# Splitting the branch, output, gate and down projections of a two-block transformer kernel into high and low parts

## What is computed

```python
# first block, each of 2 layers (x: 256 x 1024)
h = x @ w_in                                  # for three attention branches a, b, c
ya, yb, yc = moba(...), mla(...), diff(...)   # 256 x 512 each, gated with silu of a part of h
g = sigmoid(x @ w_m + b_m)                    # 1024 x 3072
merged = ga * (ya @ w_a) + gb * (yb @ w_b) + gc * (yc @ w_c)      # w_a, w_b, w_c: 512 x 1024
out = merged @ w_o                            # 1024 x 1024
r = ALPHA * x + out
r = r + sigmoid(r @ w_pg) * (p_i @ w_p)       # w_pg: 1024 x 1024
x = layernorm(r)
# second block, each of 2 layers
x = x + hybrid_mixer(rmsnorm(x))              # convolutions, a state space scan, w_in_2, w_out_2
x = x + (silu(h @ w_gate) * (h @ w_up)) @ w_down     # layer 0: dense FFN, w_down: 2816 x 1024
x = x + moe(h)                                # layer 1: top 2 of 8 experts
```

## Time and profile before

| | |
|---|---|
| time, median of 3 runs | 2277.96 us (2274.99 to 2281.9) |
| profiled execution | 2279.82 us, span of its trace 2277.6 us |
| TensorE matmul busy | 2223.8 us, 98% of the span |
| VectorE, ScalarE, GpSimd busy | 1355.2, 1200.6, 455.5 us |
| mean granted TensorE clock | 0.984 of full speed |

### The profile page before, as it was taken

How to read it: one execution, slowest core, us unless ns; L and a number is a source line. 1 busy time by engine, 2 the same in 40 slices (tenths; PEclk the granted TensorE clock), 3 DMA queues, 4 the chain that set the end, 5 groups by cost and what they waited for, 6 DMA issues and landing times.

```text
span 2277.6 us, 32486 instructions
## 1 busy us (share of the span) xinstructions
PE 2223.8 (98%) x12804; PEld 1953.8 (86%) x12804; DVE 1355.2 (60%) x1365; ACT 1200.6 (53%) x1296; POOL 455.5 (20%) x224
## 2 busy tenths in 40 slices
PE   9999999999999999999998999999999999999997
PEld 8979998988998898999897888888888888888885
DVE  1454212335311693000593898998989898989895
ACT  4456213455421543222442676777777676767673
POOL 6626412725530201445300000000000000000000
PEclk9999999999999999999998999999999999999998
DMA  7434444615444334545435798999999999999992
GB/s 233 123 113 144 151 163 147 184 44 177 148 156 148 121 104 132 180 148 186 133 110 185 283 371 326 378 354 348 371 326 368 334 373 329 369 329 374 358 352 101
DMA packets 306510, 528.26 MB, mean 232 GB/s; under 512 B 11376, under 2 KB 152336, under 8 KB 306416
## 3 DMA queue, kind: packets, MB, share of 16 engines
q1 hardware_dynamic: 306224, 526.44, 66.2%
q0 software_dynamic: 192, 0.48, 0.1%
HBM read 525.84 MB, written 1.05 MB: 231 GB/s over the span
## 4 chain that ended last, share of the span: by engine, by line
PE 86%; issue 5%; DVE 3%; POOL 3%; ACT 2%; DMA 1%; DVEq 0%; POOLq 0%; ACTq 0%
PE bank L631 83%; POOL weights_low L2516 2%; PE bank L1242 1%; DVE qb L1873 1%; ACT sc L1344 1%; DVE sc L1873 1%; PE bank L783 0%; DMA ring<-in_w_out_dram 0%; ACT weights_high L1347 0%; PE bank L686 0%; DVE h L1881 0%; DVE expert_weights_low L1873 0%; DMA ring<-in_ffn_w_up_dram 0%; DVE sc L1881 0%; ACT expert_weights_high L1347 0%
## 5 line engine op out<-in xcount | busy, mean ns | idle before, releaser
L1873 DVE TENSOR_TENSOR expert_weights_low<-ring_experts,expert_weights_high 128x2048 fp32r<-128x2048 f32 x336 | 765.2, 2289 | 94.1 <-ACT expert_weights_high L1347 93.5
L1347 ACT ACTIVATE expert_weights_high<-ring_experts 128x2048 fp32r<-128x2048 f32 x336 | 645.4, 1922 | 176.9 <-PE bank L631 176.9
L2516 POOL TENSOR_TENSOR weights_low<-ring,weights_high 128x1024 fp32r<-128x1024 f32 x176 | 429.7, 2468 | 629.8 <-ACT weights_high L1347 629.8
L1347 ACT ACTIVATE weights_high<-ring 128x1024 fp32r<-128x1024 f32 x216 | 221.2, 1054 | 381.0 <-PE bank L631 122.2
L631 PE MATMUL bank<-expert_weights_high,gathered_high 128*128 128x512 f32 x896 | 356.6, 398 | 1.4 <-DVE gathered_low L1873 1.4
L631 PE MATMUL bank<-expert_weights_high,gathered_low 128*128 128x512 f32 x896 | 349.4, 390 | 0.0
L631 PE MATMUL bank<-x_high,weights_high 128*128 128x256 f32 x896 | 256.4, 288 | 0.9 <-POOL weights_low L2516 0.9
L631 PE MATMUL bank<-x_low,weights_high 128*128 128x256 f32 x896 | 250.2, 285 | 0.0
L631 PE MATMUL bank<-x_high,weights_low 128*128 128x256 f32 x896 | 249.7, 280 | 0.0
L631 PE MATMUL bank<-expert_weights_low,gathered_high 128*128 128x512 f32 x896 | 239.7, 389 | 0.0
L631 PE MATMUL bank<-h_high,weights_high 128*128 128x256 f32 x704 | 202.7, 290 | 6.3 <-ACT h_high L1347 6.3
(11 more groups left out here) (264 smaller groups left out, 3136.5 us busy)
## 6 DMA issues: line engine op xcount, KB each, us to landing
ring_experts<-in_moe_w_gate_dram SPq DMA_DIRECT2D x112, 1024.0 KB, 6.4
ring_experts<-in_moe_w_up_dram SPq DMA_DIRECT2D x112, 1024.0 KB, 6.2
ring_experts<-in_moe_w_down_dram SPq DMA_DIRECT2D x112, 1024.0 KB, 5.8
ring<-in_w_in_dram SPq DMA_DIRECT2D x62, 1024.0 KB, 5.3
ring<-in_w_merge_dram SPq DMA_DIRECT2D x24, 1024.0 KB, 5.2
ring<-in_w_out_dram SPq DMA_DIRECT2D x16, 1024.0 KB, 5.1
ring<-in_ffn_w_gate_dram SPq DMA_DIRECT2D x11, 1024.0 KB, 5.4
ring<-in_ffn_w_up_dram SPq DMA_DIRECT2D x11, 1024.0 KB, 5.5
```

The costliest lines, as they stand in the source:

```text
L1347: return nc.scalar.activation(dst, src, ACT.Copy, scale=scale)
L1873: return nc.vector.tensor_tensor(dst, x, z, op)
L2516: nc.gpsimd.tensor_tensor(half_of(wlo[:, q_slot, :], t), half_of(ring[:, slot, :], t), half_of(whi[:, q_slot, :], t).bitcast(F32), ALU.sub ...
```

## The change

Six more kinds of weights become split units: `w_a`, `w_b`, `w_c`, `w_out`, `w_pg` of both layers and `ffn_w_down_2`. That is 14 units a layer and 11 in the FFN, 39 together. Their activations are split too: `y` into `yh`, `yl`; `merged` into `mh`, `ml`; `r1` into `xh`, `xl`; the hidden tile into `hfh`, `hfl`. `w_out_2` of the mixer stays plain. The core of the diff, with its new functions:

```diff
-          + [f"{z}z{n}" for z in "abc" for n in range(2)] + [f"mg{j}" for j in range(12)])
+          + [f"{z}z{n}" for z in "abc" for n in range(2)]
+          + [x for c, br in enumerate("abc") for x in [f"mg{4 * c + j}" for j in range(4)] + [f"b{br}0", f"b{br}2"]]
+          + [f"ou{j}" for j in range(4)] + [f"pg{j}" for j in range(4)])
-KINDS1 = [["split" if name in ("w_in", "w_merge") and cols == 256 else "plain" for name, _, cols, _ in units]
+SPLIT_WEIGHTS = ("w_in", "w_merge", "w_a", "w_b", "w_c", "w_out", "w_pg")
+KINDS1 = [["split" if name in SPLIT_WEIGHTS and cols in (256, 512) else "plain" for name, _, cols, _ in units]
...
-        kinds2 = ["split" if cols == 256 and name in ("w_in_2", "ffn_w_gate_2", "ffn_w_up_2") else "plain"
+        kinds2 = ["split" if name in ("w_in_2", "ffn_w_gate_2", "ffn_w_up_2", "ffn_w_down_2") and cols != 8 else "plain"
...
+            def split_half(b, half, slot, lo_at, x, count):
+                wh, wl = (w[:, slot, :].rearrange("p (k n) -> p k n", n=512) for w in (whi, wlo))
+                pe.wait_ge(lo_done.h, lo_at + half)
+                for t in range(2):
+                    cols = slice(half * S + t * P, half * S + (t + 1) * P)
+                    for kk in range(4):
+                        mm(views(b)[:, t, :], wh[:, kk, cols], x[0][:, kk, :], kk == 0, False)
+                        mm(views(b)[:, t, :], wh[:, kk, cols], x[1][:, kk, :], False, False)
+                        ins = mm(views(b)[:, t, :], wl[:, kk, cols], x[0][:, kk, :], False, kk == 3)
...
-                        project(name, w[:, :, 256 * (j % 2):256 * (j % 2) + 256], y[:, 4 * c:4 * c + 4, :], 4)
+                        split_half(begin(name), j % 2, *halves)
+                    elif name == "ou0":
+                        split_project_first(begin(name), *take_split(name, (mh, ml)),
+                                            lambda j: pe.wait_ge(mh_ready.h, mh_ready.at(layer, j + 1)),
+                                            lambda j: pe.wait_ge(ml_ready.h, ml_ready.at(layer, j + 1)))
+                    elif name == "pg0":
+                        split_project_first(begin(name), *take_split(name),
+                                            lambda j: pe.wait_ge(rh_ready.h, rh_ready.at(layer, j + 1)),
+                                            lambda j: pe.wait_ge(rl_ready.h, rl_ready.at(layer, j + 1)))
...
+            def down(slot, lo_at, h_at, x):
+                wh, wl = (w[:, slot, :].rearrange("p (k n) -> p k n", n=D) for w in (whi, wlo))
+                for half in range(2):
+                    pe.wait_ge(lo_done.h, lo_at + half)
...
+                            mm(views(4 + t // 2)[:, half, :], wh[:, kk, cols], hfh[:, x, kk, :], False, False, share=True)
...
ACT, in split1: what frees a half of a weight slot
+                    if half_width(before) == S:
+                        other = half_width((SPLIT1 + SPLIT1)[q]) != S
+                        G1.wait_full(act, turn, before[:2] + str(int(before[2]) + (1 if other else t)))
+                    elif half_width((SPLIT1 + SPLIT1)[q]) == S:
+                        G1.wait_full(act, turn, before)
...
ACT
+                def branch_high(n, c):
+                    act.wait_ge(gated.h, gated.at(layer, n))
+                    copy(yh[:, part, :], y[:, part, :]).then_inc(y_high.h, 1)
+                def pair_high(dst, src, ready, n, done, j):
+                    act.wait_ge(ready.h, ready.at(layer, n))
+                    copy(dst[:, 2 * j:2 * j + 2, :], src[:, 2 * j:2 * j + 2, :]).then_inc(done.h, 1)
...
+                after("bc0", (0,))
+                pair_high(mh, merged, mgd, 5, mh_ready, 0)
+                after("bc0", (1,))
+                pair_high(mh, merged, mgd, 6, mh_ready, 1)
+                after("bc2", (0,))
+                pair_high(mh, merged, mgd, 7, mh_ready, 2)
+                pair_high(mh, merged, mgd, 8, mh_ready, 3)
+                after("bc2", (1,))
                 for j in range(4):
+                    if j:
+                        after(f"ou{j - 1}", (1,))
+                    if j < 3:
+                        after(f"ou{j}", (0,))
                     drain(layer, f"ou{j}", ou[:, 2 * j:2 * j + 2, :], 0.5)
+                    if j:
+                        pair_high(xh, r1, r_ready, j, rh_ready, j - 1)
+                pair_high(xh, r1, r_ready, 4, rh_ready, 3)
+                after("ou3")
...
DVE
+                def pair_low(dst, src, high, ready, done, j):
+                    dve.wait_ge(ready.h, ready.at(layer, j + 1))
+                    tt_(dst[:, pair, :], src[:, pair, :], high[:, pair, :].bitcast(F32), ALU.subtract).then_inc(done.h, 1)
...
                         tt_(dst, dst, u, ALU.add).then_inc(mgd.h, 1)
+                        if c == 2 and j:
+                            pair_low(ml, merged, mh, mh_ready, ml_ready, j - 1)
+                    if c == 0:
+                        branch_low(3, 1)
+                pair_low(ml, merged, mh, mh_ready, ml_ready, 3)
...
DVE, FFN
-                stt(hf[:, half], tb[:, half], 0.5, views(b + 1), ALU.mult, ALU.mult).then_inc(ff_h.h, 1)
+                stt(hf[:, half], tb[:, half], 0.5, views(b + 1), ALU.mult, ALU.mult).then_inc(ff_raw.h, 1)
+                dve.wait_ge(ff_raw.h, step)
+                nc.vector.tensor_copy(hfh[:, half], hf[:, half]).then_inc(ff_high.h, 1)
+                dve.wait_ge(ff_high.h, step)
+                tt_(hfl[:, half], hf[:, half], hfh[:, half].bitcast(F32), ALU.subtract).then_inc(ff_h.h, 1)
```

More of the change, by code:

```diff
@@ L236, with half_of, half_width @@
           + [(f"wo{j}", "v") for j in range(4)])
-def half_of(unit, t):
-    return unit.rearrange("p (k t n) -> p t k n", t=2, n=P)[:, t]
+def half_of(unit, t, n=P):
+    return unit.rearrange("p (k t n) -> p t k n", t=2, n=n)[:, t]
+def half_width(name):
+    return S if name[:2] in ("ba", "bb", "bc") else P
 def quarter(unit, k):
@@ L723, in take_split @@
                     assert SPLIT1[q] == name
-                    return q % 2, lo_done.at(layer, 2 * q + 1), (xh, xl), full
+                    return q % 2, lo_done.at(layer, 2 * q + 1), x, full
                 def begin(name):
@@ L897, in layer_body @@
                         if j % 2 == 0:
[L898 removed]
+                            halves = take_split(name, (yh[:, 4 * c:4 * c + 4, :], yl[:, 4 * c:4 * c + 4, :]))
                         if j == 0:
[L900 to L907 removed]
+                            pe.wait_ge(y_split.h, y_split.at(layer, {"a": 1, "c": 2, "b": 3}[name[1]]))
+                        split_half(begin(name), j % 2, *halves)
[7 more added lines that the diff above has]
+                                            lambda j: pe.wait_ge(rl_ready.h, rl_ready.at(layer, j + 1)))
+                    elif name[:2] == "ou":
+                        split_project(begin(name), *take_split(name, (mh, ml)))
                     elif name in ("lm", "lv"):
                         b = begin(name)
[L910 removed]
                         src, ready = (merged, r2_ready) if name == "lm" else (sq, ln_sq)
@@ L1116, in norm, with take_down @@
                     pe.wait_ge(nrm["h"].h, n - 1)
[L1118 to L1124, removed]
+            def down(slot, lo_at, h_at, x):
+                wh, wl = (w[:, slot, :].rearrange("p (k n) -> p k n", n=D) for w in (whi, wlo))
+                for half in range(2):
+                    pe.wait_ge(lo_done.h, lo_at + half)
+                    if half == 0:
+                        pe.wait_ge(ff_h.h, h_at)
+                    for t in range(half, DT, 2):
+                        cols = slice(t * P, (t + 1) * P)
+                        for kk in range(2):
+                            mm(views(4 + t // 2)[:, half, :], wh[:, kk, cols], hfh[:, x, kk, :], False, False, share=True)
+                            mm(views(4 + t // 2)[:, half, :], wh[:, kk, cols], hfl[:, x, kk, :], False, False, share=True)
+                            ins = mm(views(4 + t // 2)[:, half, :], wl[:, kk, cols], hfh[:, x, kk, :], False, False,
+                                     share=True)
+                    ins.then_inc((used if half == 0 else ff_down).h, 1)
+            def take_down(x, step):
+                slot, lo_at, _, _ = take_split(ff_down)
+                down(slot, lo_at, step, x)
             def clear_sums():
@@ L1347, in copy, with split @@
                 return nc.scalar.activation(dst, src, ACT.Copy, scale=scale)
-            def split(slot, landed_at, q_slot, free, halves=(0, 1)):
+            def split(slot, landed_at, q_slot, free, halves=(0, 1), width=P):
                 act.wait_ge(landed[slot].h, landed_at)
@@ L1374, in free @@
                         G1.wait_full(act, turn, before)
-                split(n % RING, 16 * (n // RING + 1), q % 2, free, halves)
+                split(n % RING, 16 * (n // RING + 1), q % 2, free, halves, half_width((SPLIT1 + SPLIT1)[q]))
             def drain(layer, name, dst, scale=1.0, rows=slice(0, P)):
```

161 lines of the change are left out of this document (108 added, 53 removed).

## The result

The changed kernel takes 2243.25 us in the median of 4 runs (2242.33 to 2248.41), the kernel before 2276.59 beside it: a ratio of 0.9854, 95% interval 0.9832 to 0.9877. The forecast was 2242, the range 2230 to 2264. The profiled execution is the longest of the four, 2248.41 us with a span of 2246.6.

A forecast was written before the change was run, and what follows sets the result against it. TensorE's own work was taken as the bound: 2279.8 - 45.8 saved on PE + 10 of new waits = 2244.0 us for the profiled execution, 2242 in the median. Range 2230 to 2264 us.

The forecast's parts named there:

- The bound and the price of a block: PE's own work sets the time; a block costs 431.7 ns plain, 359.7 (layers) or 354.9 (FFN) split; 45.8 us less.
- the 119.9 ns: Price of one fp32r matmul, read from mg8 to mg11 (192 in 23.02 us); three make a split block, 359.7 ns.
- The price by four passes and three quarters: All plain matmuls: three products cost three quarters of float32's four passes, 67.3 us less, 2221 us; chance 0.02.
- What is given back: PE waits at three places a layer as DVE and POOL exclude each other: 5 us a layer, 10 both, bounds 0 and 16.
- ou0: First output unit: PE waits for its weights and the last pair of merged, 3 us a layer.
- the walk with the two engines in turn: Wait at the first output unit, walked through with measured durations, DVE and POOL alternating: 3 to 4 us.
- pg0: First gate unit: its second weight half and the chain from ou3 come late, between 0 and 2, taken as 1 us.
- The end of the gate groups: Two DVE operations after pg3 meet POOL on the next layer's first weights: between 0 and 2.4, taken as 1 us.
- B, collisions that fall well: POOL and DVE miss each other at the three places, PE waits about 1 us in all, 2233 us; chance 0.18.
- C, POOL as the bound: From bc0 to pg3 POOL's halves pace the units, up to 21 us over 20 units, 2250 to 2264 us; chance 0.20.
- D: Slower: POOL halves above 3.45 us in all 39 units; at 4 us each, 43 us slower, 2320 us; chance 0.06.
- E: No measurable difference: POOL halves of 3.3 to 3.5 us, 2271 to 2285 us; chance 0.04.

The follow-up runs named there:

- port_free: Changed kernel with DVE's two-SBUF-tile operations from the last branch to the gate groups reading a bank instead (other values computed); bc0 to norm's sums 57.7 us against 62.9.
- the fillers: Changed kernel with 6 and 3 bf16 matmuls of zeros before PE's waits for high pairs 2 and 3 of merged; 2236.64 us, ratio 0.9834.
- lows_last: Changed kernel with DVE making the low parts of merged behind its last add of bc3, not between the adds; 2236.48 us, ratio 0.9817.
- copies_first: Changed kernel with ACT copying pairs 2 and 3 of merged before it splits ou1's first weight half; 2246.72 us, ratio 0.987.

## Why the prediction was right, point by point

**The bound and the price of a block** held. TensorE's work set the time. The FFN gained 13.3 us (forecast 13.5). In the layers, with the waits taken out (`ou0` to `pg0` in `port_free`, the rest in the changed kernel, `bc0` to `ou0` less 1.02 us of waiting for weights), each gained 2.46 + 2.45 + 2.45 + 4.84 + 4.90 = 17.1 us, 34.2 for both against 32.3. That term was 2 us too small: the 119.9 ns were read over a stretch that begins just behind plain matmuls, with a first one of 0.47 us. Behind split units the same four gate units take 22.83 us instead of 23.02, and a whole branch unit pair 11.36 us, 118.3 ns a matmul. Together 47.5 us instead of 45.8. The price by four passes and three quarters, the rival at 2221 us, is excluded: a loop turn of split units alone takes 34.08/288 = 118.3 ns a matmul.

**What is given back** was the right mechanism, in the right places, and too small: 10 us forecast with bounds of 0 and 16, and 18.1 measured in the profiled execution, outside its own bounds.
- `ou0`: 3 us a layer forecast; 1.0 for the weights and 4.9 in the output groups (27.70 - 22.79) measured, 5.9. The waits themselves are 3.5 us, within what the walk with the two engines in turn gave (3 to 4). Another 1.5 us is the half clock on 24 matmuls, which the sum did not have at all; the fillers gave 1.4 of it back. The rest, some 0.9 us, is slower starts behind each wait and the wait before `pg0`.
- `pg0`: 1 us a layer forecast, 0.3 measured, before its first matmul; it is contained in the 4.9 above.
- The end of the gate groups: 1 us a layer forecast; 0.6 in layer 0, but 2.8 + 2.7 in layer 1. There two units are split ahead and not one, so POOL is at work through DVE's last operations: the pair before the last ends 1 us late, and the last operation of all takes 2.71 us instead of 0.69. Behind that the clock halves again, and this is the whole of the second 2.7: the 16 squares take 6.23 us instead of 3.53. A window of the changed kernel in layer 1:

```profile
730.00:735.00 5.00, 5.00 (x13) 3.97 (x12) 0.47 (x1) 2.42 (x3) 0.00 (x0) 0.50 0.12 7
```

So the half clock, which stood nowhere in the sum, is 1.5 + 1.5 + 2.7 = 5.7 of the 18.1 us. With the port taken out (`port_free`) the clock stayed up and the same stages gave back only 1.7 us: nearly all of the loss comes of DVE's lateness at the port, directly or by the clock behind it.

**Why the total came out** nearly exact all the same: the profiled execution is 31.0 us shorter in its span. Of this -47.5 + 18.1 = -29.4 are the change's, where the forecast had -45.8 + 10 = -35.8. The start took 3.0 us more, mixer 0 and 1 took 4.3 and 0.9 less, the experts 0.6 more. The second execution of the same kernel has its start at 228.66 and its mixer at 161.47, so these are chance. The agreement of the medians to 1 us is luck: two terms were off by 2 and 8 us, which together is 6.4 us too much gain, and executions of one kernel differ by more than that.

**The rivals.** B, collisions that fall well, did not come: four operations in a row were held up, in both layers and in both executions, so it is the program's order and not luck. C, POOL as the bound, did not either: its median is 2.40 us, its longest 3.41 as before, and PE waits for low weights 0.8 us by name and 2.1 us under `issue`. It was near, though: from 324.39 POOL did six halves without a pause in 16.00 us, 5.33 a unit against PE's 5.7. The FFN stayed at PE's pace with a margin that was used: `hidden_low` took 2.8 to 2.9 us in each step. D and E are excluded by the interval.

## What to carry to other kernels

A helper engine that was idle is a cover like any other: when POOL is given work all the time, each VectorE operation on two SBUF tiles may cost 2 to 3 us instead of 0.7, and those on the way to the next matmul should be counted one by one, with the order in which the two engines meet. Put such operations behind the ones that somebody waits for, or let them read a bank. Look where they go: moved behind the norm, POOL's work met DVE's scaling and nothing was won. And price a wait of TensorE with the clock it may cost behind it, which here was 1.5 us behind waits of 3.5.

## What the runs showed of the hardware that was not expected

- Behind three waits of 0.9, 1.9 and 0.7 us within 7.3 us TensorE's clock fell to 1.2 GHz for most of 4.3 us; nine matmuls of zeros in those waits kept it at 2.4 GHz, and the kernel 0.8 to 1.4 us a layer shorter in these groups. Behind waits of 0.87 and 0.96 us (`lows_last`) and of 0.86, 0.36 and 0.71 us (`copies_first`) in the same unit it did not fall.
- Of 11 subtractions of the hidden tile none took less than 2.77 us: in a loop in which two engines keep one order, the collision was not a chance, it happened each time.
- Executions of one kernel differ by up to 16 us, in step with their mean granted clock (2235.59 us at 0.989, 2251.68 at 0.980).
